# Late modulation and norm rows held as columns and spread by TensorE, and six weight pieces of the tail loaded once

## The reference, cut to what matters

```python
def ada_mod(c, w, b):
    shift, scale, gate = jnp.split(jax.nn.silu(c) @ w + b, 3, axis=-1)
    return shift[:, None, :], 1.0 + scale[:, None, :], 1.0 + gate[:, None, :]

for i in range(DEPTH):
    shift, scale, gate = ada_mod(c, ada_w[i, 0], ada_b[i, 0])
    h = x * scale + shift
    f = short_conv_mixer(...) if i % 2 == 0 else diff_attention(...)
    x = layer_norm(DEEPNORM_ALPHA * x + gate * f, ln_g[i, 0], ln_b[i, 0])
    shift, scale, gate = ada_mod(c, ada_w[i, 1], ada_b[i, 1])
    h = x * scale + shift
    f = peer_ffn(h, peer_w_q[i], peer_sub_keys[i], peer_u[i], peer_v[i])
    x = layer_norm(DEEPNORM_ALPHA * x + gate * f, ln_g[i, 1], ln_b[i, 1])

def peer_ffn(h, w_q, sub_keys, u, v):        # 8 heads, 128 x 128 keys, top 16
    ...                                       # idx, g: 128 experts for each token
    act = gelu(einsum('td,thkd->thk', xc, u[idx]))
    return einsum('thk,thkd->td', g * act, v[idx])
```

## Time and profile before

| | |
|---|---|
| median of 3 runs | 2801.14 us (2797.15 to 2802.27) |
| the profiled execution | 2799.27 us, span 2797.5 us |
| granted TensorE clock, mean | 0.984 |
| busy share PE / PEld / DVE / ACT / POOL | 91% / 57% / 54% / 23% / 24% |
| chain that ended last, by engine | PE 65%, DMA 21%, DVE 8%, ACT 3% |
| DMA moved | 942.59 MB, mean 337 GB/s |
| gathers | 512, 1 MB each |
| tail weight pieces | 55, 1 MB each |

### The profile page before, as it was taken

How to read it: one execution, slowest core, us unless ns; L and a number is a source line. 1 busy time by engine, 2 the same in 40 slices (tenths; PEclk the granted TensorE clock), 3 DMA queues, 4 the chain that set the end, 5 groups by cost and what they waited for, 6 DMA issues and landing times.

```text
span 2797.5 us, 26838 instructions
## 1 busy us (share of the span) xinstructions
PE 2533.8 (91%) x9923; PEld 1592.6 (57%) x9923; DVE 1523.4 (54%) x3481; ACT 634.6 (23%) x1837; POOL 682.6 (24%) x723
## 2 busy tenths in 40 slices
PE   8999999999999999999899777999879989777776
PEld 6874558847884688668665323645426646332222
DVE  4552144514550545513778975365795666974445
ACT  2001210001000210000233333343333533332222
POOL 1110001100110002200243544243443333543332
PEclk9999999999999999999999999999999999999999
DMA  9994427954893359856899999999999999999997
GB/s 384 383 368 161 164 101 278 362 207 156 340 363 132 133 199 386 353 199 234 326 404 421 421 421 421 413 417 421 421 417 406 421 421 414 422 401 422 421 421 323
DMA packets 123321, 942.59 MB, mean 337 GB/s; under 512 B 15886, under 2 KB 17318, under 8 KB 22583
## 3 DMA queue, kind: packets, MB, share of 16 engines
q0 software_dynamic: 95392, 673.29, 58.9%
q1 hardware_dynamic: 27798, 267.60, 24.4%
HBM read 939.72 MB, written 1.11 MB: 336 GB/s over the span
## 4 chain that ended last, share of the span: by engine, by line
PE 65%; DMA 21%; DVE 8%; ACT 3%; issue 1%; POOL 1%; SPq 0%; DVEq 0%
PE psW L947 20%; DMA ring<-in_peer_uv_dram,lamt 20%; PE psF L1294 13%; PE psF L865 11%; PE psW L1397 4%; DVE ring L2467 3%; PE psW L835 2%; PE psW L805 2%; PE psW L794 2%; PE psW L1313 1%; PE psF L893 1%; PE psW L846 1%; PE psW L1409 1%; DMA mring<-in_tail_w_dram 1%; PE psF L1164 1%
## 5 line engine op out<-in xcount | busy, mean ns | idle before, releaser
L1294 PE MATMUL psF<-ring,p_diag 128*128 128x512 f32 x2048 | 963.0, 616 | 212.4 <-ACT p_diag L1713 212.3
L2467 DVE SCALAR_TENSOR_TENSOR ring<-ring,h 128x1024 f32<-128x1024 f32 x512 | 620.8, 1224 | 423.6 <-DMA ring<-in_peer_uv_dram,lamt 420.2
L652 POOL DMA_INDIRECT ring<-in_peer_uv_dram,lamt x512 | 577.8, 1129 | 1001.0 <-PE psF L1294 809.7
L1294 PEld LDWEIGHTS psF<-ring,p_diag 128*128 128x128 f32 x2048 | 382.5, 195 | 737.6 <-issue 394.4
L947 PE MATMUL psW<-hT,ring 128*128 128x256 f32 x2560 | 553.2, 379 | 0.0
L947 PEld LDWEIGHTS psW<-hT,ring 128*128 128x128 f32 x2560 | 487.1, 190 | 64.9
L865 PE MATMUL psF<-ring,arena 128*128 128x512 f32 x704 | 303.2, 593 | 4.0 <-DVE arena L2132 4.0
L865 PEld LDWEIGHTS psF<-ring,arena 128*128 128x128 f32 x704 | 133.7, 190 | 171.8 <-issue 166.2
L484 POOL DMA_DIRECT2D mring<-in_mod_t_dram x80 | 42.5, 532 | 731.1 <-DVE mring L1996 727.0
L1706 ACT ACTIVATE small<-small 128x2 f32<-128x2 f32 x255 | 51.6, 202 | 654.2 <-DVE ring L2467 653.8
L1713 ACT ACTIVATE p_diag<-ident,small 128x128 f32<-128x128 f32 x510 | 176.9, 394 | 8.3
(11 more groups left out here) (324 smaller groups left out, 2184.8 us busy)
## 6 DMA issues: line engine op xcount, KB each, us to landing
ring<-in_gu_t_dram SPq DMA_DIRECT2D x44, 2048.0 KB, 9.1
mring<-in_mod_t_dram POOLq DMA_DIRECT2D x80, 1024.0 KB, 7.6
mring<-in_tail_w_dram SPq DMA_DIRECT2D x50, 1024.0 KB, 9.1
M<-in_mod_t_dram POOLq DMA_DIRECT2D x40, 1024.0 KB, 7.8
ring<-in_down_t_dram SPq DMA_DIRECT2D x20, 2048.0 KB, 9.4
ring<-in_conv_in_t_dram SPq DMA_DIRECT2D x12, 2048.0 KB, 7.4
ring<-in_gla_in_t_dram SPq DMA_DIRECT2D x6, 2048.0 KB, 7.8
ring<-in_out_t_dram SPq DMA_DIRECT2D x6, 2048.0 KB, 7.7
```

Of the source, the lines that this page charges most:

```text
L652: pool.indirect_dma_start(out=pair(n % PAIRS), out_offset=None, in_=rows, in_offset=bass.IndirectOffsetOnAxis(ap=s_idx[:, c:c + 1], axis=0 ...
L1294: ins = pe.matmul(psF[:, b, f * HALF:(f + 1) * HALF], p_diag[:, n % PAIRS, :], row_v(n % PAIRS)[:, f * HALF:(f + 1) * HALF], start=(i == 0 ...
L2467: dve.scalar_tensor_tensor(row_u(c), row_u(c), 1.0, h[:, b, :], ALU.mult, ALU.mult, accum_out=p_dots[:, c:c + 1]).then_inc(dot_done, 1)
```

## The change

- `ROWS` loses the five rows (8, 2), (9, 2), (10, 0), (10, 1), (10, 2). Their sums stay in SBUF as columns (`LATE`, `late_col`), 8 numbers on each partition; the norm rows of the tail come as columns too (`ln_col`, one small load `ln_cols` at the start). `norm_rows` is gone from SyncE's queue; the conv's norm rows are still broadcast.
- `late_row` on TensorE spreads a column: 8 transposes, each with one number of every partition repeated 128 times as the stationary operand, fill a row of 1024 in two banks. `row_first` is `psW[0]` and `psW[1]`, `row_second` is `psW[2]` and `psM`; the four banks are now one tensor `psR`.
- ScalarE copies a gate out of `row_second` into `h[:, b, :]` (`copy_gate`), so that ln_b can take its place. VectorE reads ln_g, ln_b, scale and shift from PSUM (`late_normalise`, `prepare_block`).
- In `attend` the spreading stands at steps 0, 1 and 2, in step 28, and at 30, 31 and 33. What stood at 33 and later on TensorE (turning h, keys, queries, scores, choice) stands one step later on TensorE, ScalarE and VectorE. Phase 3 gets `last_rows`.
- The room that `M_at`, `M_p1` and the rows took holds weight pieces: `KEPT` names six of the 24 pieces (0, 3, 6, 9, 11, 18) that are loaded once for both halves. Pieces 3, 6 and 9 are sent for among the conv's weights; 0, 11 and 18 during phase 0. The other 18 pass through the two homes of `mring` twice (`PASSING`).
- Small moves: `t_qT`, `s_sum`, the gate of the last norm (`last_gate`).

The diff, cut to its core:

```diff
+KEPT = {6: 5, 3: 6, 9: 7, 0: 4, 11: 8, 18: 3}
+PRELOADED = (3, 6, 9)
+PASSING = [(b, c) for b in range(2) for c in range(CHUNKS) if c not in KEPT]
-ROWS = ((0, 2), (1, 2), (2, 2), (5, 2), (8, 1), (4, 2), (6, 2), (7, 2), (8, 2), (9, 2), (8, 0), (10, 0), (10, 1), (10, 2))
+ROWS = ((0, 2), (1, 2), (2, 2), (5, 2), (8, 1), (4, 2), (6, 2), (7, 2), (8, 0))
+LATE = {(8, 2): (0, 0), (9, 2): (0, 1), (10, 0): (1, 0), (10, 1): (1, 1), (10, 2): (2, 0)}
...
+                if st is conv7 and j in (2, 3, 4):
+                    load_kept(PRELOADED[j - 2])
                 fill(st.w + j)
...
+        load_kept(0)
+        load_kept(11)
+        for n in range(len(PASSING)):
+            load_passing(n)
+            if n == 1:
+                load_kept(18)
...
+        def late_row(ps, column):
+            for k in range(KD):
+                ins = pe.transpose(ps[:, k * P:(k + 1) * P], column[:, k:k + 1].to_broadcast([P, P]), ident[:])
+            ins.then_inc(late_row_full, 1)
...
+            yield from pause(clock, 0)
+            pe.wait_ge(d_stored, d_units.n)
+            late_row(row_second, late_col(8, 2))
+            yield from pause(clock, 1)
+            have_a(a_units.n)
+            late_row(row_first, ln_col[:, 0, 0, :])
+            yield from pause(clock, 2)
+            pe.wait_ge(gate_copied, 2 * b + 1)
+            late_row(row_second, ln_col[:, 0, 1, :])
...
                 output(i)
+                if i == 2:
+                    pe.wait_ge(d_stored, d_units.n)
+                    late_row(row_second, late_col(9, 2))
+            yield from pause(clock, 30)
+            have_a(a_units.n)
+            late_row(row_first, ln_col[:, 1, 0, :])
+            yield from pause(clock, 31)
+            pe.wait_ge(gate_copied, 2 * b + 2)
+            late_row(row_second, ln_col[:, 1, 1, :])
             yield from pause(clock, 33)
+            pe.wait_ge(x_done, 2 * b + 2)
+            late_row(row_first, late_col(10, 1))
+            late_row(row_second, late_col(10, 0))
+            yield from pause(clock, 34)
             turned = turn_a(h, b)
-            yield from pause(clock, 34)
+            yield from pause(clock, 35)
...
+        def copy_gate(dst, made):
+            act.wait_ge(late_row_full, made)
+            act.activation(dst, row_second, ACT.Copy).then_inc(gate_copied, 1)
...
+            yield from pause(clock, 1)
+            copy_gate(h[:, b, :], 8 * b + 1)
...
+            yield from pause(clock, 30)
+            copy_gate(h[:, b, :], 8 * b + 4)
...
+        def late_normalise(b, made):
+            dve.wait_ge(late_row_full, made)
+            dve.wait_ge(var_ready, t_var.n)
+            link(dve.scalar_tensor_tensor(x[:, b, :], x[:, b, :], lnag[:, b, 0:1], row_first, ALU.subtract, ALU.mult))
+            return scaled(b, row_second)
...
             yield from pause(clock, 33)
-            prepare_block(b, M_p1)
-            yield from pause(clock, 38)
+            dve.wait_ge(late_row_full, 8 * b + 8)
+            prepare_block(b, row_first, row_second)
+            yield from pause(clock, 39)
```

More of the change, by code:

```diff
@@ L254, in _program @@
     s_e = gains[:, 320:384].rearrange("p (s n) -> p s n", s=2)
-    s_sum = gains[:, 384:386]
+    s_sum = small[:, 88:90]
+    last_gate = arena[:, 2048:3072]
+    t_qT = [[v.rearrange("p (a t) -> p a t", a=2) for v in pieces]
+            for pieces in ((M[:, 0, 2, 512:768], M[:, 0, 2, 768:1024]), (gains[:, 384:640], arena[:, 6144:6400]))]
     s_g = gout[:].rearrange("p (b n) -> p b n", b=TB)
@@ L309, in _program @@
     d_stored = sem("d_stored")
-    chunk_loaded = [sem(f"chunk_loaded{i}") for i in range(5)]
+    chunk_loaded = [sem(f"chunk_loaded{i}") for i in range(9)]
     o_used = sem("o_used")
@@ L331, in _program, with first_chunk, block_chunk @@
     chunk_homes = [mring[:, 0].rearrange("p k n -> p (k n)"), mring[:, 1].rearrange("p k n -> p (k n)"),
[L332 to L348, removed]
+                   arena[:, 0:2048], arena[:, 4096:6144], M[:, 0, 0:2].rearrange("p v n -> p (v n)"),
+                   arena[:, 6400:8448], arena[:, 8448:10496], arena[:, 10496:12544], arena[:, 12560:14608]]
+    def first_chunk(n):
+        return n % 4, n // 4 + 1
+    def block_chunk(b, c):
+        if c in KEPT:
+            return KEPT[c], 3 if KEPT[c] < 4 else 1
+        n = PASSING.index((b, c))
+        return n % 2, 2 + n // 2 + 1
     last = stages[-1]
@@ L691, in _ @@
                 pool.wait_ge(x_ready, x_count(6))
-                norm_rows(pool, 7, conv_ln_loaded)
+                for j, name in enumerate(("ln_g_2", "ln_b_2")):
+                    pool.dma_start(ln[:, j, :], a[name][0, 0:1, :].to_broadcast([P, D])).then_inc(conv_ln_loaded, 16)
             if piece:
@@ L1282, in scores_a @@
             for j in range(4):
-                ins = pe.matmul(ps[:, j * P:(j + 1) * P], t_qT[:, buf, j, :], t_skT[:, j % 2, :], start=True, stop=True)
+                ins = pe.matmul(ps[:, j * P:(j + 1) * P], t_qT[buf][j // 2][:, j % 2, :], t_skT[:, j % 2, :],
+                                start=True, stop=True)
             ins.then_inc(a_full, 1)
@@ L1522, in attend, with last_rows @@
                 asked = queries
[L1523 removed]
+            yield from pause(clock, 43)
             scores_a(1, asked)
             assert a_units.n == base + BLOCK_UNITS
+        def last_rows():
+            clock = Turn()
+            yield from pause(clock, 0)
+            pe.wait_ge(d_stored, d_units.n)
+            late_row(row_second, late_col(10, 2))
+            yield from pause(clock, 1)
+            have_a(a_units.n)
+            late_row(row_first, ln_col[:, 2, 0, :])
+            yield from pause(clock, 2)
+            pe.wait_ge(gate_copied, 5)
+            late_row(row_second, ln_col[:, 2, 1, :])
         def tail():
[L1528 removed]
+            beside = [first_queries(), attend(0), attend(1), last_rows()]
+            pe.wait_ge(col_stored, 4 + 2 * len(PIECES))
+            pe.wait_ge(misc_loaded, 16 * MISC)
             first_groups()
@@ L1883, in attend @@
                     scores(hd // 2 - 1)
-            yield from pause(clock, 43)
+            yield from pause(clock, 44)
             scores(3)
@@ L1893, in finish_first @@
             clock = Turn()
+            yield from pause(clock, 1)
+            copy_gate(last_gate, 17)
             yield from pause(clock, 2)
@@ L2714 @@
         [columns(v).reshape(P, -1) for v in bias] + [columns(v).reshape(P, -1) for v in gains], axis=1))
+    given["ln_cols"] = np.ascontiguousarray(np.concatenate(
+        [columns(inputs[name][n // 2, n % 2]).reshape(P, -1) for n in range(1, 4) for name in ("ln_g_2", "ln_b_2")], axis=1))
     def tile(w):
```

180 lines of the change are left out of this document (83 added, 97 removed).

## The result

The changed kernel takes 2813.07 us in the median of five runs (2809.38 to 2815.99), the kernel before 2799.1 (2797.15 to 2802.27): ratio 1.0047, 95% interval 1.0037 to 1.0058. I had forecast 2789 with a range of 2774 to 2806, so the change went the other way and past the range.

A forecast was written before the change was run, and what follows sets the result against it. Transfers bound phases 1 and 2 on average, with TensorE or VectorE full in some steps. Phase 0 +5.0, phase 1 -14, phase 2 -3.3 sum to -12.3: 2799.3 becomes 2787, forecast as a median of 2789 (own range 2781 to 2797, overall 2774 to 2806).

The forecast's parts named there:

- The choice: Choice of experts, steps 43 to the end: VectorE's waits for gathers go, -10.1 us in phase 1, -5.5 in phase 2.
- second rival: Nothing gained behind the first half, as the choice's waits on short dependent passes only change their name: 2803 us, chance 0.22.
- The hand-over: Steps 28 to 35: queries start later but one more step is done, net +4.3 us in phase 1, +2.5 in phase 2.
- The start of phase 2: First steps of phase 2: three rows among the slots and the norm's wait for the gate cost +4.4 us.
- Steps 5 to 25: Phase 1: TensorE's idle time, 5.3 us in steps 5 to 17 and 5.3 in 18 to 25, goes: -10.6 us.
- The late piece's 4.16 us: Phase 1, steps 5 to 17: TensorE's one wait for late piece 6, 4.16 us, goes because the piece now stays.
- Phase 0: Transfers are never idle in phase 0, so two more units (pieces 11 and 18) cost +5.0 us.
- the preload is hidden: Three pieces among the conv's weights cost nothing under TensorE; the rival, conv waiting 7.5 us, gave 2796, chance 0.04.
- the dear rows: Rival that spreading is dear: 3.3 us a row instead of 0.9, 13 rows waited for, 2820 us, chance 0.10.
- the slower case: The rival that spreading a row costs 3.3 us, giving 2820 us, chance 0.10.
- the first rival: All ten units come back because TensorE's and VectorE's full stretches had slack: 24.8 us less, 2776, chance 0.22.
- the -14 that I took for -15.5: Phase 1 in all: -15.5 us by the engines, -14.9 by transfers; entered as -14, two close limits not both being met.

The follow-up runs named there:

- exp43: Changed kernel with ScalarE's first exponential of each choice put ahead of the last query piece's copy: 2813.15 us, ratio 1.0042 to the kernel before.
- skipgather: Changed kernel with every second gather of steps 44 to 63 in phases 1 and 2 replaced by a plain transfer of a sixteenth: 2804.21 us.
- again: Changed kernel loading the kept pieces 3, 6, 9, 11 and 18 a second time for the second half: 2818.31 us, ratio 1.0059 to the kernel before.
- fewer: Kernel before with pieces 3, 6, 9, 11 and 18 of each half loaded only to a sixteenth: 2787.46 us, ratio 0.9949.
- warm: Changed kernel with 48 extra unread transposes of the identity behind the modulation rows: 2808.38 us, ratio 1.0022 to the kernel before.
- rows32: Changed kernel with the two modulation rows spread behind step 32's slots instead of step 33's: 2797.64 us, ratio 0.9984 to the kernel before.

## Why the prediction was wrong

The sum was -12.3, the profiled executions differ by +10.1: 22.4 us, which I find in these terms (differences of the table's rows).

- **The choice: forecast -10.1 and -5.5 beside a step less (5.0 each), measured -8.6 and -4.8. This step failed, by 12.2 us.** I took VectorE's waits for gathers as waits that go when pieces go. But no piece goes in this stretch: 44 gathers are issued in it before and 42 after, at 2.484 us 109.3 and 104.3 us, and of pieces one of the next half in phase 1 and none in phase 2, in both kernels. 107.5 and 106.2 stand 2 to 3 us above that. exp43 (without ScalarE's wait nothing changes), skipgather (with fewer gathers the stretch shrinks) and again (one piece more costs one unit) show it. What phase 1 gained beside the step, 3.7 us, came from ahead of the stretch: it moved 3.4 MB less, of which the step's two gathers are 2.1, so more had landed in the buffers when it began. fewer gained 3.8 and 1.6 us there in the same way; phase 2 of the changed kernel gained nothing. My second rival was right that these waits stay, though not in its 2803, and its reason was wrong: the chain of short passes and replies is the next limit, at 102.4 us in skipgather.
- **The hand-over: forecast +9.3 in phase 1 and +7.5 in phase 2 with its further step, measured +13.7 and +11.4.** Place, order and VectorE's wait (7 us forecast, 8.4 measured) were right. What I left out is the clock: I entered the slots of steps 33 and 34 at 3.6 us, and they take 5.40 and 6.11, which is 4.3 us more and nearly all of the 4.4 missing in phase 1. Before has slots of 6.54 us there too (the 9.97 for 16 in the earlier trace rows); I read the row and did not ask why. warm shows the cause for step 34; what lowered the clock ahead of step 33 stays open.
- **The start of phase 2: +4.4 forecast, +7.0 measured.** VectorE's wait for the gate is 5.3 us instead of 3, and the slots of step 4 behind it take 5.40. The same start takes 25.55 us in rows32 and 25.96 in again, whose edits do not touch it, with 3.70 in step 4, so part of the 7.0 is spread between executions.
- **Steps 5 to 25: -10.6 forecast in phase 1, -6.8 measured; -5.0 in steps 18 to 25 of phase 2, -3.8 measured.** The late piece's 4.16 us went. In steps 18 to 25 of phase 1, 4.7 of TensorE's 5.3 idle us stayed, and VectorE waits 23.0 us for gathers in steps 18 to 29 after and 23.4 before. No run took gathers away there, so that they are the limit here too is only likely.
- **Phase 0: +5.0 forecast, +1.8 measured**; the eleven kernels that preload have 349.0 to 353.5 us, median 351.5, against 347.6 and 348.5 in before and fewer, so the size is nearer 3.5.
- **Right:** the preload is hidden (phase 0 begins 0.24 us later; over all kernels its beginning has a median of 1362.2 us with the preload and 1362.9 without); the row in step 28 costs 0.88 and 0.99 us against 0.9; steps 5 to 17 of phase 2 stay, at 94.3; passes that read a row from PSUM take 1280 ns against 1285. The Trainium skill, "TensorE: Matmul & The Clock Gate", section "Part 4: PE-mode transpose", gives about 275 ns for a transpose of 128x128 in bf16 within a kernel; the 152 transposes of the rows, in f32, last

```profile
L1310 PE MATMUL psR<-ident,small x152: 272/273/273, 1714.2 to 2498.4; 128*128 128x128 f32 x152
```

and still stand 0.11 us apart, so the dear rows are refuted: the slower case came, but not by its mechanism. TensorE was rightly taken as full in steps 5 to 17, against the first rival.

Phase 3 gave 1.5 us that I had not counted, and the -14 that I took for -15.5 hides 1.5 more. My slower case had the wrong place: the hand-over stood in the sum as +4.3 and +2.5, yet I gave it no rival of its own.

## What to carry to other kernels

A wait for a transfer becomes shorter by transfers that stand in the same stretch, and by those ahead of it only as far as the buffers can hold what is gained: count what each stretch moves by kind before crediting a saving from elsewhere. Where a new wait makes TensorE idle, price the multiplications behind it at the lower clock as well, and make what the other engine waits for ahead of the work that is itself waiting. Between two limits a few us apart, an edit that removes one measures as nothing until the other is moved.

## What the runs showed of the hardware

A gather of 64 rows of 8 KB onto 64 partitions kept the DMA engines as busy as one of 128 rows: 207 GB/s against 422 at the same share of 1.01. And 48 transposes that nobody reads made the kernel 4.7 us faster (7.0 by the ratios), with TensorE's granted clock at 1.00 across a wait of 6 us and in the slots behind it.
